# Null products on TensorE ahead of the first operands, two more weight tiles split in quarters, and the first sums of squares one step later

## What is computed

```python
def first_block(x, ...):
    for i in range(2):
        h = rmsnorm(x, g[0])
        m = hyena_shortconv_mixer(h, ...) if i == 0 else pool_mixer(h, ...)
        x = x + rmsnorm(m, g[1])
        h = rmsnorm(x, g[2])
        x = x + rmsnorm(jnp.square(jax.nn.relu(h @ mlp_w1[i])) @ mlp_w2[i], g[3])
    return x

def hyena_shortconv_mixer(h, w_in, ..., f_w1, f_b1, f_w2, f_b2, f_w3, f_b3, freq, hy_bias, ...):
    z = h @ w_in                       # (256, 2048) @ (2048, 6144)
    ...                                # short convolutions, gates
    h_fwd, h_bwd = hyena_filters(...)  # emb @ f_w1 -> sin -> @ f_w2 -> sin -> @ f_w3
    ...                                # long convolution through a DFT

def second_block(x, mem, ...):         # attention of three kinds, then an output projection
```

## Time and profile before

| what | us |
|---|---|
| median of 3 runs | 2379.53 |
| lowest and highest | 2373.3, 2380.79 |
| profiled execution | 2376.94 |
| its span | 2375.1 |
| TensorE busy (PE) | 2347.8 (99%) |
| VectorE busy (DVE) | 1323.5 (56%) |
| ScalarE busy (ACT) | 1098.5 (46%) |
| DMA, mean | 188 GB/s |

### The profile page before, as it was taken

How to read it: one execution, slowest core, us unless ns; L and a number is a source line. 1 busy time by engine, 2 the same in 40 slices (tenths; PEclk the granted TensorE clock), 3 DMA queues, 4 the chain that set the end, 5 groups by cost and what they waited for, 6 DMA issues and landing times.

```text
span 2375.1 us, 25347 instructions
## 1 busy us (share of the span) xinstructions
PE 2347.8 (99%) x10971; PEld 1946.5 (82%) x10971; DVE 1323.5 (56%) x1336; ACT 1098.5 (46%) x1180; POOL 25.7 (1%) x45
## 2 busy tenths in 40 slices
PE   8999999999999999999999999999999999999998
PEld 6778788888888888888888888888888888888887
DVE  5665855544544544556764454454554585656754
ACT  6444444654354354354555434434434365534443
POOL 0000000000000000000000000000000010000000
PEclk9999999999999999999999999999999999999999
DMA  8445455555555555555555555555555545643443
GB/s 308 161 165 183 180 195 195 211 180 194 195 196 194 195 180 192 195 180 210 202 188 184 189 194 186 188 193 187 188 192 187 191 167 194 233 156 142 148 152 144
DMA packets 63903, 446.07 MB, mean 188 GB/s; under 512 B 7241, under 2 KB 7572, under 8 KB 12143
## 3 DMA queue, kind: packets, MB, share of 16 engines
q1 hardware_dynamic: 61312, 429.58, 50.8%
q0 software_dynamic: 2336, 14.76, 1.7%
q10 hardware_dynamic: 144, 0.12, 0.0%
HBM read 442.33 MB, written 2.10 MB: 187 GB/s over the span
## 4 chain that ended last, share of the span: by engine, by line
PE 93%; DMA 3%; DVE 2%; ACT 2%; issue 1%; POOL 0%; SPq 0%; ACTq 0%; POOLq 0%
PE P L334 90%; PE P L337 3%; DVE raw_r L584 1%; ACT hi L471 1%; DMA raw<-in_w_i 1%; DMA raw<-in_w_z 1%; DMA raw<-in_w_d 0%; DMA raw<-in_w_ukv 0%; DVE R_h L571 0%; ACT R_h L467 0%; DVE R_m L568 0%; DMA raw<-in_w_o 0%; ACT EV L497 0%; DVE X L571 0%; POOL st L910 0%
## 5 line engine op out<-in xcount | busy, mean ns | idle before, releaser
L584 DVE TENSOR_TENSOR raw_r<-raw,hi 128x2048 fp32r<-128x2048 f32 (+3 forms) x421 | 930.1, 2211 | 952.4 <-ACT hi L471 951.1
L471 ACT ACTIVATE hi<-raw 128x2048 fp32r<-128x2048 f32 (+3 forms) x421 | 778.2, 1850 | 1015.5 <-DMA raw<-in_w_d 389.7
L334 PE MATMUL P<-hi,R_h 128*128 128x512 f32 (+2 forms) x3840 | 1227.3, 394 | 12.9 <-DVE raw_r L584 9.8
L334 PEld LDWEIGHTS P<-hi,R_h 128*128 128x128 f32 x3840 | 721.7, 188 | 164.3 <-issue 13.9
L334 PE MATMUL P<-hi,R_f_r 128*128 128x512 f32 x2480 | 777.3, 391 | 0.7 <-DVE raw_r L584 0.7
L334 PE MATMUL P<-raw_r,R_h 128*128 128x512 f32 (+2 forms) x1920 | 745.5, 388 | 0.0
L334 PEld LDWEIGHTS P<-hi,R_f_r 128*128 128x128 f32 x2480 | 465.5, 188 | 97.6 <-DVE raw_r L584 1.4
L334 PE MATMUL P<-raw_r,R_f_r 128*128 128x512 f32 x1240 | 482.6, 389 | 0.0
L334 PEld LDWEIGHTS P<-raw_r,R_h 128*128 128x128 f32 x1920 | 361.7, 188 | 73.5 <-issue 4.3
L334 PEld LDWEIGHTS P<-raw_r,R_f_r 128*128 128x128 f32 x1240 | 232.9, 188 | 47.5
L337 PE MATMUL P<-ident,EV 128*128 128x128 f32 (+1 forms) x478 | 71.7, 272 | 1.7 <-ACT EV L467 0.6
(11 more groups left out here) (189 smaller groups left out, 809.5 us busy)
## 6 DMA issues: line engine op xcount, KB each, us to landing
raw<-in_w_u SPq DMA_DIRECT2D x128, 1024.0 KB, 4.8
raw<-in_w_d SPq DMA_DIRECT2D x128, 1024.0 KB, 4.8
raw<-in_w_z SPq DMA_DIRECT2D x47, 1024.0 KB, 4.8
raw<-in_w_i SPq DMA_DIRECT2D x36, 1024.0 KB, 4.8
raw<-in_w_mo SPq DMA_DIRECT2D x16, 1024.0 KB, 4.9
raw<-in_w_o SPq DMA_DIRECT2D x16, 1024.0 KB, 4.7
raw<-in_w_mkv SPq DMA_DIRECT2D x8, 1024.0 KB, 4.7
R_g<-in_rows POOLq DMA_DIRECT2D x6, 1024.0 KB, 5.1
```

The source lines that it names most:

```text
L334: return self.e.matmul(o, l, r, start=start, stop=stop, skip_group_check=True)
L471: self.e.activation(hi, raw, ACT.Copy).then_inc(*self.inc("high_made", ("high", k, d)))
L584: self.e.tensor_tensor(low, raw, hi.bitcast(f32), ALU.subtract).then_inc(*self.inc("low_made", *names))
```

## The change

Four things change in `conduct`, with two small functions for the first:

- `warm`: VectorE fills the staging tile EV1 with zeros, and TensorE multiplies it with itself three times into the bank P5, ahead of its first product. The results are not used. Tile and bank are taken from their rotations, so each later user of a staging tile or small bank gets the next one.
- Tiles 2 and 3 are split in quarters between the column blocks 8 to 15, as tiles 0 and 1 were. The count of tiles that are already split starts at 4.
- `half_squares` comes one step later, behind one more `nop`; `first_norm` too.
- By that everything in `extra` comes one step later as well: the small matmul of `filter_1` at the end of tile 3 where it was in its middle, that of `filter_2` at the end of tile 7 where it was in its middle. The transposes keep their places (from the middle of tile 5, and from the middle of tile 8). From the 23rd tile on the order of TensorE is as it was, but for the numbers of tiles and banks.

```diff
--- before.py
+++ after.py
@@ -324,7 +324,7 @@
         gated_silu = gated_v = gates = half_dft = half_silu = halved_rstd = halves = head_columns = inverse = load_piece = load_tile = \
         masked_exp = memory_out = mla_out = nsa_out = ones_row = plain_exp = plain_parts = padded_keys = pool_scale = pool_windows = \
         product = norm_mean = norm_root = relu_square = residual = rope = rope_keys = scale = scaled_parts = scores = side_load = side_taps = sine = \
-        split = square_sum = store = times_row = turn = v_times_k = values = y_back = idle
+        split = square_sum = store = times_row = turn = v_times_k = values = warm = y_back = idle
 
 
 class Pe(Engine):
@@ -347,6 +347,13 @@
         if k == 3:
             last.then_inc(*self.inc("product_done", done))
 
+    def warm(self, b, k, n, zero, done):
+
+        self.wait_ge(zero)
+        for _ in range(n):
+            last = self.mm(self.m.P[b][:, :], self.m.EV[k][:, 0:128], self.m.EV[k][:, :], True, True)
+        last.then_inc(*self.inc("turn_done", done))
+
     def turn(self, outs, ins, ready, free, done):
         self.wait_ge(free)
         self.wait_ge(ready)
@@ -585,6 +592,9 @@
 
     def cols_ready(self, m):
         self.wait_ge(m)
+
+    def warm(self, b, k, n, zero, done):
+        self.e.memset(self.m.EV[k][:, :], 0.0).then_inc(*self.inc("dve_done", zero))
 
     def halves(self, done):
         self.e.memset(self.m.half[:, :], -0.5).then_inc(*self.inc("dve_done", done))
@@ -1320,6 +1330,9 @@
     E.first_load("c4", m.cols[:, 0:a["cols"].shape[1]], a["cols"], id_m[0])
     half_m = mark("halves")
     E.halves(half_m)
+    b, k, warmed = bank(), ev(), mark("warm")
+    E.warm(b, k, 3, mark("zero"), warmed)
+    bank_free[b] = ev_free[k] = [warmed]
 
     def first_tile(d):
         q = slice(1024 * d, 1024 * d + 1024)
@@ -1382,15 +1395,11 @@
     for g in range(4):
         for c in range(4):
             first_column(4 * g + c)
-            if g < 2:
-                q = slice(512 * c, 512 * c + 512)
-                E.split(g, c, m.hi[g][:, q], m.raw[g][:, q], m.low[g][:, q], True)
-        if g == 1:
-            at_["high"] = 0 if listing else 2
-        elif g == 2:
-            split_ahead(3)
+            q = slice(512 * c, 512 * c + 512)
+            E.split(g, c, m.hi[g][:, q], m.raw[g][:, q], m.low[g][:, q], True)
+    at_["high"] = 0 if listing else 4
     fl = {}
-    later += [nop, last_rows, half_squares, nop, first_norm]
+    later += [nop, last_rows, nop, half_squares, nop, first_norm]
 
     def sine(b, ready, cb, o):
         done = mark("sine")
```

## The result

| what | before | after |
|---|---|---|
| median of 7 runs, us | 2376.66 | 2383.68 |
| lowest and highest | 2373.3, 2380.79 | 2382.78, 2385.44 |
| profiled execution | 2376.94 | 2383.96 |
| its span | 2375.1 | 2382.2 |

The ratio of after to before is 1.0026, with a 95% interval of 1.0017 to 1.0036: slower, by 7.0 us, a size just under the 0.3% (7.1 us) that the prediction set as its bound. The forecast was 2388 with a range of 2382 to 2394.

What follows compares the result with a forecast made beforehand. TensorE, running nearly without a gap, was taken to bound the kernel. 2376.9 plus 7.0 us for the moved steps and 4.2 for two clock falls made 2388.1, predicted as 2388 us, range 2382 to 2394.

Steps and rivals of the forecast that it cites:

- The moved steps were the cost: First two transpose groups: later filter sines delay evacuations; transposes at 44.7 and 67.8 us, loss 2.8, then 7.0 us.
- its early bound: First transposes: the end of ScalarE's squares allows them at most 0.3 us earlier than 44.7.
- None of this depends on the null products: First transposes: 44.7 us comes from the landing of tile 6, whatever the null products do.
- The start: First tiles: hidden null products lift the clock, the 0.60 us wait at tile 2 goes; TensorE 2.4 us ahead.
- The clock in the waits: Behind both long transpose waits: clock falls to half, costing 2.1 us each, 4.2 together, ends 0 and 5.4.
- Rival (a): Both transpose waits come, but the clock falls in one or none: 2386.0 or 2383.9 us; chance 0.21.
- The sum of the first 80 us: Start through second transposes: 7.0 us from the moved steps plus 4.2 us from clock falls.
- The rest of the program: Behind the second transposes: shifted filter_3 products and DFT pairs are hidden, cost nothing, bounds 0 and about 1 us.
- (b): Only the first transpose wait comes, as the split of tile 10 is done in time: 2381.8 us; chance 0.07.
- (c): Start's gain is kept because group 0's evacuation starts before 37.9: 2374.5 us; chance 0.05.
- (d): Null products fail to lift the clock: TensorE about 0.5 us ahead, same forecast time; included in the forecast's 0.65.

Runs made afterwards that it cites:

- e6: The changed kernel with one nop fewer, so filter_2 is back at its old step and filter_1 stays late; 2378.41 us, ratio 1.0006 to before.
- e4: The changed kernel with four and five float32 null products directly ahead of the first transposes of groups 0 and 1; 2383.63 us, ratio 1.0031 to before.
- e1: The kernel before with only the extra nop that moves the steps, no null products, no quarters; 2384.83 us, ratio 1.0031 to before.
- e3: The changed kernel with half_squares still late but the second nop removed, so the filters keep their old steps; 2374.49 us, ratio 0.9993 to before.
- e2: The changed kernel with the old queue of steps, null products and quarters kept; 2374.41 us, ratio 0.9988 to before.
- e7: The changed kernel with the old queue of steps and five null products instead of three; 2373.51 us, ratio 0.9989 to before.
- e12: The kernel before with only filter_1 and filter_2 moved behind the transposes of groups 0 and 1; 2376.70 us, ratio 0.9994 to before.
- e8: The changed kernel with old steps for the squares, five null products and both filters behind their group's transposes; 2372.22 us, ratio 0.9980 to before.
- e10: The kernel before with only the three null products and the fill of their tile; 2374.24 us, ratio 0.9983 to before.

## Why the prediction was right

Point by point, by its own steps.

**The moved steps were the cost: right, and by the named mechanism.** Predicted 44.7 for the first transposes, measured 44.30; ScalarE starts the split of tile 6 at 36.03 (predicted 36.3) and each later distance is the one read from before to within 0.1 us. What set 36.03 was the end of the squares, which the prediction had as its early bound, and not the landing of tile 6, from which it said that 44.7 comes. That landing came at 35.6: issued 1.6 us earlier than before (26.0 for 27.6), it landed 0.7 us earlier, where the prediction took no gain at all. In e6 the landing was late and did set the instant, in e4 that of tile 5 did; both moved the transposes by 1.5 to 2 us. For the second, 67.8 was predicted without the clock; measured is 69.09, of which 1.6 us are the first fall, so 67.5. That it is the sine's new place: e1 (the steps alone cost everything), e3 (late squares with the filters in place cost nothing), e6 (put one sine back and its wait goes).

**"None of this depends on the null products": right.** e1 has its first transposes at 43.96 without them. The waits were 3.90 and 4.94 us instead of 5.4 and 4.9, since TensorE came to the first at 40.4 and not 39.3.

**The start: half right.** The null products are hidden, and the wait of tile 2 went. I took the clock as up from the first real product; in after it was at 0.50 behind the gap of 2.07 us between the null products and the first real one, and TensorE was 1.6 us ahead behind the filter product (31.93 against 33.5) instead of 2.4. The gap was in the row I used: three products that end by 4.5 to 7.5 leave up to 3 us open. This had no price, since all of it was waited away at 44.30.

**The clock in the waits: right in kind, too large in size.** Both falls came, 0.50 behind each. I took 2.1 us each between 1.6 (worked out from 3.3 us at 1.2 GHz) and 2.7; measured are 1.6 (4.81 - 3.20) and 1.6 (4.82 - 3.21), 3.2 in all for 4.2. (Half of the start's 5.7 us is 2.85 and not 2.7; the slip moves nothing.) The nearer row, the fall late in the program, was the right one; the start was not. Rival (a) was no idle one at such lengths: the clock fell behind 2.78 us in e2 and 2.79 in e7, and not behind 2.76 in e3 and in e12. Behind the waits of 3.90 us and more (after, e1, e6) it was down each time. The Trainium skill ("TensorE: Matmul & The Clock Gate", "What's actually happening") says that the chip's look at activity runs free and is not reset by the kernel, so the place of a change of clock varies; e2 and e3 are in keeping with it (4.76 and 3.22 us behind the same wait).

**The sum of the first 80 us** was 11.2 us and came out as 9.8; 1.0 of the 1.4 us are the falls. **The rest of the program**, which I cost at nothing, gave 2.7 us back in the profiled execution. So 2388.1 became 2383.96: 1.4 us from sizes at the start and 2.7 from a stretch that the prediction left out because the change doesn't touch it. It had its row: the 2.29 us wait was quoted for its clock and never asked whether it would still be there. Between medians (before 2376.66 here, 2377.5 to 2377.8 beside the experiments) after is 6 to 7 us slower, and not 9.8, so part of the give-back seems to hold on average too. With it the size fell just under "slower by over 0.3%", to which I had given 0.76, into "within it", to which I had given 0.19. And the place in the range is in part luck: both waits and both falls came, for which the lower bound was 2384, and 2383.68 is inside only because the range had been drawn down to 2382 for rival (a), which did not come.

**Rivals.** (b), only one wait, fell: both came. (c) named the right condition (evacuation start before 37.9): it started at 42.92, and in e8, where it starts at 38.32, the time does fall below before, though most of that in the late stretch. (d) was half true at the start and changed nothing, as it said.

## What to carry to other kernels

A step that is moved by one place in a queue moves everything behind it: list what each follower stands in front of on every in-order engine, and look for an evacuation that TensorE waits for. A start that is ahead is worth only what the next fixed instant lets through: here 1.6 us ahead behind tile 3 were gone at the transposes. A part that the change doesn't touch can still move: a load late in the program landed in 4.9 us where it had taken 6.5. Before a give-back of 0.1% there is explained, look how far executions of one kernel scatter, and set the medians beside the profile.

## What was not expected of the hardware

- The granted clock can fall between null products and the real ones: it was down behind a gap of 2.07 us (after), and the first product was at full speed behind gaps of 0.68 (e2), 1.16 (e10) and 1.35 us (e6). Three null products lasted between 4.27 us (after) and 5.49 us (e3) as merged rows, so the gap differs between executions of like code.
- The same wait had two outcomes for the clock, 2.78 us with a fall and 2.76 us without, and a wait of 1.90 us at 1936.64 in e7 had one behind it (granted clock 0.50 from 1938 us); the price of a fall was 1.5 to 1.6 us where it could be read behind the transposes.
- A load of 1 MB landed in 6.5 to 7.4 us in four kernels and in 4.8 to 5.5 us in ten, at the same place of one program.
- One kernel scatters by 6 us between executions, and its time goes with its mean granted clock.
